# Reordering tile 0 of a hybrid decoder step on one Trainium2 core: gate projection, leaf scores, sink terms, last square sum

## The reference

```python
u = _rmsnorm(h, norm_g)
gla, g_gate, (sq, sk, sv), s_gate = _project(u, w_in, w_gate_up, b_gate)
o_gla, S = _gla_branch(*gla, s0, gla_norm)        # gated linear attention, S_t = diag(a_t) S_{t-1} + k_t v_t^T
o_swa, k_new, v_new = swa_fn(sq, sk, sv)          # softmax over 128 keys back, one learned sink per head
h = h + _merge(o_gla, g_gate, o_swa, s_gate, w_out)   # concat(o * silu(gate)) @ w_out
```

## Time and profile before

| | us |
|---|---|
| median of 3 runs | 915.76 (914.79 to 916.89) |
| the profiled execution | 914.17 |
| its span, from first to last instruction | 912.4 |
| TensorE busy | 885.8 |
| VectorE busy | 688.4 |
| ScalarE busy | 382.9 |
| GpSimd busy | 77.0 |
| mean granted TensorE clock | 0.970 |

### The profile page before, as it was taken

One profiled execution on the slowest core, in us unless ns is written; L12 is line 12 of the kernel. 1 busy time (PEld: TensorE's weight loads), 2 busy tenths in 40 slices (PEclk: granted clock), 3 DMA queues, 4 the chain that ended last, 5 costly groups with the idle time before them and its releaser, 6 DMA issues.

```text
span 912.4 us, 22426 instructions
## 1 busy us (share of the span) xinstructions
PE 885.8 (97%) x9066; PEld 617.6 (68%) x9066; DVE 688.4 (75%) x2223; ACT 382.9 (42%) x1008; POOL 77.0 (8%) x114
## 2 busy tenths in 40 slices
PE   7897999999999999999999999999999999999987
PEld 5874567585857676675858576676758576765855
DVE  5899586877777778868787777878687777786743
ACT  4555353435353343435353433534353534435311
POOL 0041010101010010101010000101010100101400
PEclk8998999999999999999999999999999999999776
DMA  9922002020010202020100202020200102020221
GB/s 378 369 94 70 1 2 93 1 85 10 24 71 2 93 1 94 2 94 1 67 28 17 77 2 94 2 93 1 94 2 34 61 2 93 3 73 24 77 110 39
DMA packets 15686, 56.55 MB, mean 62 GB/s; under 512 B 3745, under 2 KB 5209, under 8 KB 14560
## 3 DMA queue, kind: packets, MB, share of 16 engines
q1 hardware_dynamic: 15296, 55.05, 16.0%
q10 hardware_dynamic: 288, 0.07, 0.0%
HBM read 44.33 MB, written 10.78 MB: 60 GB/s over the span
## 4 chain that ended last, share of the span: by engine, by line
PE 87%; DVE 8%; DMA 2%; issue 2%; ACT 1%; SPq 0%; DVEq 0%
PE bank L570 24%; PE bank L571 23%; PE bank L572 23%; PE bank L763 3%; PE bank L677 2%; PE bank L810 2%; PE bank L689 2%; PE bank L783 2%; PE bank L787 1%; DMA w_out_lo<-in_w 1%; DVE w_in_hi_lo L1717 1%; PE bank L749 1%; PE bank L624 1%; PE bank L798 1%; DMA x_rows<-in_xq 1%
## 5 line engine op out<-in xcount | busy, mean ns | idle before, releaser
L570 PE MATMUL bank<-u_hi,w_in_hi_lo 128*128 128x128 f16 (+1 forms) x1288 | 208.4, 215 | 3.6 <-DVE w_in_hi_lo L1717 2.8
L571 PE MATMUL bank<-u_lo,w_in_hi_lo 128*128 128x128 f16 (+1 forms) x1288 | 208.0, 214 | 0.0
L572 PE MATMUL bank<-u_hi,w_in_hi_lo 128*128 128x128 f16 (+1 forms) x1288 | 208.0, 214 | 0.0
L571 PE MATMUL bank<-w_in_hi_lo,u_hi 128*128 128x512 f16 (+3 forms) x528 | 175.8, 342 | 0.0
L572 PE MATMUL bank<-w_in_hi_lo,u_lo 128*128 128x512 f16 (+3 forms) x528 | 175.7, 341 | 0.0
L570 PE MATMUL bank<-w_in_hi_lo,u_hi 128*128 128x512 f16 (+3 forms) x528 | 175.5, 342 | 0.0
L570 PEld LDWEIGHTS bank<-u_hi,w_in_hi_lo 128*128 128x128 f16 x1288 | 124.0, 98 | 16.2 <-issue 13.0
L571 PEld LDWEIGHTS bank<-u_lo,w_in_hi_lo 128*128 128x128 f16 x1288 | 123.8, 98 | 0.3
L572 PEld LDWEIGHTS bank<-u_hi,w_in_hi_lo 128*128 128x128 f16 x1288 | 123.7, 98 | 0.0
L570 PE MATMUL bank<-w_out_hi,ogT_hi 128*128 128x512 f16 x256 | 98.7, 386 | 1.5 <-DVE ogT_lo L1638 1.5
L571 PE MATMUL bank<-w_out_lo,ogT_hi 128*128 128x512 f16 x256 | 98.5, 385 | 0.0
(11 more groups left out here) (296 smaller groups left out, 1747.8 us busy)
## 6 DMA issues: line engine op xcount, KB each, us to landing
xT<-in_xT SPq DMA_DIRECT2D x16, 512.0 KB, 4.9
x_rows<-in_xq SPq DMA_DIRECT2D x16, 512.0 KB
flex<-in_w SPq DMA_DIRECT2D x4, 2048.0 KB, 10.6
flex<-in_xq SPq DMA_DIRECT2D x16, 512.0 KB, 4.0
out_y<-flex SPq DMA_DIRECT2D x16, 512.0 KB, 2.6
w_out_lo<-in_w SPq DMA_DIRECT2D x2, 2048.0 KB, 12.3
w_out_hi<-in_w SPq DMA_DIRECT2D x1, 2048.0 KB, 10.1
w_out_hi<-in_w SPq DMA_DIRECT2D x1, 1088.0 KB, 7.2
```

Of the source, the lines that this page charges most:

```text
L570: nc.tensor.matmul(out, a_hi, b_hi, start=start and i == 0, stop=False)
L571: nc.tensor.matmul(out, a_hi, b_lo, start=False, stop=False)
L572: mm = nc.tensor.matmul(out, a_lo, b_hi, start=False, stop=stop and i == last)
```

## The change

In tile 0 only, TensorE makes the gate projection gg ahead of the values of units 0 and 1 (before: behind the turns of units 2 and 3), and the leaf scores ahead of the turns of units 2 and 3 (before: behind gg). sg follows the turns. On VectorE the addition of the sinks is cut out of `denominators` into `sink_steps`; in tile 0 it now stands ahead of `factors`, in all other tiles where it was. In the preparation of the weights, the square sum of the eighth piece now stands ahead of both halves of the low part of the seventh (before: between them). No instruction is added or taken away.

```diff
                 if early:
                     proj(nxt, "gv")
+                    proj(t, "gg")
                 else:
                     proj(nxt, "sklow")
                     proj(nxt, "gv", 4)
                 values(t, 0)
                 values(t, 1)
+                if early:
+                    leaf_scores(t)
                 turn_probs(t, 2)
                 turn_probs(t, 3)
                 if early:
-                    proj(t, "gg")
-                leaf_scores(t)
-                if early:
                     proj(t, "sg")
                 else:
+                    leaf_scores(t)
                     proj_rest(nxt, "gv", 4)
...
-            def denominators(t):
+            def sink_steps(t):
                 at_ring.wait_freed(dve, "s3", t)
                 V.tensor_tensor(wst[:, 2, :], wst[:, 0, :], sink[:, :], ALU.add).then_inc(dve_w.sem, 1)
+
+            def denominators(t):
                 act_w.wait(dve, "es", t)
...
+                if i == NG - 2:
+                    square_sum(i + 1)
                 lo_w(i, 0)
                 if i < NG - 1:
-                    square_sum(i + 1)
+                    if i < NG - 2:
+                        square_sum(i + 1)
...
                 row_max(t, 3)
-                if not early:
+                if early:
+                    sink_steps(t)
+                else:
                     final_scale(t + -1)
...
                 assemble_leaves(t)
+                if not early:
+                    sink_steps(t)
                 denominators(t)
```

## The result

The changed kernel took 909.86 us (median of 5 runs, 908.8 to 911.06) against 915.76 (914.79 to 918.38) for the kernel before, run beside it: a ratio of 0.9932 with a 95% interval of 0.9912 to 0.9952, which is 4.4 to 8.1 us less. A second series gave 909.2 against 914.94, ratio 0.9935 (0.9921 to 0.9949). The forecast was 910.4. The profiled execution took 908.8 us.

A forecast was written before the change was run, and what follows sets the result against it. TensorE, busy 885.8 of 912.4 us, was taken to set the pace. Tile 0's stretch would shrink 7.07 us without clock loss, less 1.7 for a low-clock spell: 5.4 us, from 915.76 to 910.4, range 908.2 to 913.2.

The forecast's parts named there:

- Step (1): Tile 0 on TensorE: gg, ahead of the first values, waits for VectorE's drain of sq and starts at 81.64 us.
- The cover: Tile 0: while gg runs, the waits for the second pair's exponentials and leaf factors run out, saving 2.0 us.
- Step (3): Tile 0 on VectorE: sooner sink terms delay the factors by 0.2 us (0.1 to 0.4); gain and loss nothing.
- Step (4): Weight preparation: the last square sum sooner wins 0.3 us, with bounds of 0.6 won and 0.3 lost.
- Step (5): TensorE behind the idle gap: clock at 0.50 for 3.4 us of work costs 1.7 us, leaving 5.4 won.
- no fall: Upper bound for tile 0's stretch if the clock stays full behind the idle gap: 7.1 us won.
- The sum: Whole kernel: 5.4 us less, taking the median from 915.76 to 910.4 us.
- The clock never falls: Rival, chance 0.13: the clock stays full behind tile 0's idle gap, 7.1 us won, 908.7 us.
- gg doesn't wait at all: Rival, chance 0.03: in tile 0 gg's bank is free sooner, gg starts at 77.95; 7.9 us won, 907.9.
- The handed-back gain: Rival, chance 0.07: VectorE or ScalarE becomes late at third values or level scores, losing all 5.4 us; 915 to 916.

The follow-up runs named there:

- draining first: The changed kernel, with VectorE draining sq of tile 1 ahead of tile 0's decay sums: 907.37 us against 914.62 for the kernel before.
- filled gap: The changed kernel with 16 unread matmuls between the value projection and gg: 911.61 us, again 910.44; with 8 instead of 24 unread matmuls at the start, 909.37.
- gg only: The kernel before with only gg moved ahead of the first values: 912.00 us against 914.62, again 909.89 against 914.68.
- leaf scores back: The changed kernel with the leaf scores back behind the turns of the second pair: 909.48 us against 914.94 for the kernel before.
- long warm-up: The changed kernel with 40 instead of 24 unread matmuls at the program's start, gap left idle: 913.03 us against 914.68 for the kernel before.
- leaf scores only: The kernel before with only the leaf scores moved ahead of the second pair's turns, gg left behind them: 915.97 us against 914.68.
- square sum only: The kernel before with only the last square sum moved sooner: 914.08 us against 914.62, ratio 0.9993.

## Why the prediction was right

*Step (1), gg's start.* Right. It said that gg starts about when the gap ends, held by the drain of sq: 81.64. Less the 1.12 us of the opening, gg started at 81.34. That the drain is the cause is shown by draining first, which ends the wait: gg follows the value projection at once. The 0.14 us from VectorE's end to TensorE's start came out as 0.09 (81.69 + 0.68 = 82.37, gg at 82.46).

*The cover.* Right, and shown from both sides: behind gg the leaf scores and turns don't wait, and their order changes the distance by 0.01 us; without gg in front TensorE waits in either order, 2.0 us for the exponentials or 2.4 us for the leaf factors.

*Step (3).* Right: no one waited for the factors, which end at 87.32 (86.90 + 0.42), 2.8 us ahead of the leaf scores. The sink step's cost itself was not measured alone.

*Step (4), the square sum.* Mis-sized on the low side, within its bounds: 0.55 us instead of 0.3. VectorE waited 0.34 us for the gram, a little more than the 0.25 I read from the earlier trace rows, and the 0.47 us for the bound are gone (65.79 carries no wait); but the weight split (63.53) took 2.35 us and not the 2.75 of the earlier trace rows, which was the other bound: 0.47 - 0.34 + 0.40 is 0.53. The 0.40 belong to the edit, since the split took 2.35 us in all ten kernels' traces with the square sum moved and 2.75 or 2.76 in the four without; why was not tried.

*Step (5), the clock.* Right: one spell at 0.50 of about 3.4 us, a loss of 1.7. The filled gap removes the spell and wins exactly 1.70 us of distance, and its 7.36 is the bound of "no fall", 7.07, with the better square sum. The size was no luck of one execution. In all six traces in which gg starts behind an idle gap and work then goes on without a break (the change twice, gg only twice, leaf scores back, long warm-up), the clock was low for 3.4 us and eight of gg's matmuls were slow. Here is the change's second one:

```profile
82.40:85.60 3.20, 3.20 (x9) 1.18 (x8) 3.06 (x17) 1.52 (x6) 0.00 (x0) 0.50 0.00 0
```

Where the old order leaves waits behind the gap, the spell was longer: 10.1 us in the kernel before, as long in leaf scores only, and 6.7 in square sum only. That the breaks are the reason, as the prediction took it, fits these nine traces but was not tried by itself. The kernel before was profiled once, so whether its own spell varies is not known. The Trainium skill's "TensorE: Matmul & The Clock Gate", section "Part 1: The HAM clock gate", has 6, 11 or 14 slow matmuls for one kernel at its start. Behind this gap the number differed between kernels, from 5 to 12, and was the same in both traces of the change and of gg only; the slow matmuls of a start were not counted here.

*The sum.* 5.4 us forecast, 5.66 us of tile 0 measured, and 5.9 and 5.7 us by the medians of the two series. The parts agree as well. By the rows the 5.66 are 0.55 for the square sum; 0.84 because gg starts with the drain of sq (81.80 + 0.09), while the first values had to wait for PT until 82.73; 2.02 of covered waits; and 2.25 of low clock and issue (3.96 before, 1.71 now). So the largest part of the gain is the shorter spell at 0.50, and it leans on the spell of 10.1 us in the one trace of the kernel before. Against square sum only, with its 6.7 us, the rest of the change is worth 3.65 us of distance (39.80 to 36.15) instead of 5.11. The shift of tile 0 arrives at the end whole, since the tiles behind it take 50.40 us before and after. That the two profiled spans differ by just the 5.4 us forecast is chance: the changed one lost 1.12 us in its opening, and the one of before 0.9 in a single long tile.

*The rivals.* "The clock never falls" was what the filled gap makes, not the change. "gg doesn't wait at all" came true only where the drain was moved, with 8.82 us less instead of the 7.9 I gave it. The handed-back gain did not occur, but the filled gap shows the way in which it would: a late transfer of x_rows.

## What to carry to other kernels

When a stall sits on a busy engine, look first at what the piece to be put into it waits for itself: here it could not fill the gap, and won by letting the next waits run out behind it and, in these traces, by a shorter spell of low clock. Then look for the one small step that holds it back; moving that drain ahead took another 3.2 us off the distance, of which some 1.4 us show in the medians of separate series. Compare edits of a few microseconds by a distance within the trace between two marks, one ahead and one behind the edit, and only then by the time.

## What was not expected

The opening and the end vary by more than the change's parts. The clock was low for 16.6 us of the changed kernel's opening and for 10.1 in that of before, and the mark, which the reordering does not touch, stood between 59.0 and 61.1 us, latest (60.6 to 61.1) in the three traces with the longest low clock in the opening, some 17 us; the last stretch, from the loop's last final scaling to the end, took 61.3 to 64.8 us across these kernels.

The x_rows transfer, two tiles ahead, has little to spare. Where ScalarE waited up to 2.6 us for it, tiles took 50.40 us; beyond that each took longer by as much as the wait grew: 50.50 at 2.71 us, 50.81 at 3.03, 51.10 at 3.30. The kernel before had one such tile in its profiled execution (51.33 at 3.54), with the 0.8 us of the earlier trace rows. And 32 more instructions in TensorE's program, ahead of the loop, made that wait 0.5 to 1.5 us longer, twice with the gap filled and once without; with the program back at its old length it was as short as ever. The link between the two is open.
